# Expert weights loaded, waited for and released expert by expert

## What is computed

```
combine = jnp.sum(one_hot(expert_id, 16) * top_w[..., None], axis=1)
for e in range(N_EXPERTS):                       # 16 experts, 1024 -> 512 -> 1024
    he = jax.nn.silu(t @ w_gate[e]) * (t @ w_up[e])
    y = y + combine[:, e:e + 1] * (he @ w_down[e])
```

## Time and profile before

| | us |
|---|---|
| median of 3 runs | 702.59 |
| lowest and highest | 701.43, 703.89 |
| the profiled execution | 701.2 |
| its span | 699.4 |
| PE busy in the span | 662.6 (95%) |
| DVE, ACT busy | 298.5, 192.0 |

### The profile page before, as it was taken

How to read it: one execution, slowest core, us unless ns; L and a number is a source line. 1 busy time by engine, 2 the same in 40 slices (tenths; PEclk the granted TensorE clock), 3 DMA queues, 4 the chain that set the end, 5 groups by cost and what they waited for, 6 DMA issues and landing times.

```text
span 699.4 us, 9145 instructions
## 1 busy us (share of the span) xinstructions
PE 662.6 (95%) x3442; PEld 380.2 (54%) x3442; DVE 298.5 (43%) x632; ACT 192.0 (27%) x342; POOL 16.2 (2%) x29
## 2 busy tenths in 40 slices
PE   6999999999999999997999999999999999999883
PEld 5878778653444444431388878784543353352331
DVE  4478986611232122121474888673221322121234
ACT  3457543421111110100154554342201111111102
POOL 3100000200000000000020000000000000000000
PEclk9999999999999999999999999999999999999998
DMA  9985049999999999999986330998999999999991
GB/s 339 327 291 186 1 189 423 379 412 408 423 420 420 423 420 421 422 421 421 402 291 235 126 121 31 396 422 330 424 419 422 422 420 421 420 422 420 422 408 63
DMA packets 46027, 240.96 MB, mean 345 GB/s; under 512 B 3457, under 2 KB 3649, under 8 KB 21281
## 3 DMA queue, kind: packets, MB, share of 16 engines
q1 hardware_dynamic: 44800, 238.21, 84.2%
q0 software_dynamic: 1040, 2.04, 1.2%
q10 hardware_dynamic: 144, 0.13, 0.1%
HBM read 239.32 MB, written 1.05 MB: 344 GB/s over the span
## 4 chain that ended last, share of the span: by engine, by line
PE 75%; DMA 22%; DVE 1%; issue 1%; ACT 1%; DVEq 0%; SPq 0%
PE psum L1086 23%; PE psum L765 22%; DMA up_w<-in_w_up 21%; PE psum L1119 10%; PE psum L785 4%; PE psum L1066 3%; PE psum L1027 2%; PE psum L745 1%; PE psum L991 1%; PE psum L932 1%; DMA x<-in_x 1%; PE psum L1100 1%; PE psum L844 1%; PE psum L801 1%; PE psum L820 0%
## 5 line engine op out<-in xcount | busy, mean ns | idle before, releaser
L1086 PE MATMUL psum<-up_w,xT 128*64 128x512 f32 x512 | 114.2, 594 | 9.8 <-DMA up_w<-in_w_up 9.8
L1119 PE MATMUL psum<-down_w,scores 128*64 128x512 f32 x512 | 113.5, 595 | 0.0
L765 PE MATMUL psum<-piece_hi,hT_part 128*128 128x512 f32 x320 | 100.1, 394 | 0.0
L1086 PEld LDWEIGHTS psum<-up_w,xT 128*64 128x64 f32 x512 | 36.9, 137 | 83.7 <-issue 64.5
L1119 PEld LDWEIGHTS psum<-down_w,scores 128*64 128x64 f32 x512 | 36.6, 137 | 63.9 <-issue 61.6
L765 PEld LDWEIGHTS psum<-piece_hi,hT_part 128*128 128x128 f32 x320 | 59.0, 188 | 13.2 <-issue 1.7
L1523 DVE TENSOR_TENSOR y_lo<-psum,y_hi 128x512 fp32r<-128x512 f32 x32 | 22.1, 691 | 101.9 <-ACT y_hi L701 101.9
L765 PE MATMUL psum<-piece_lo,hT_part 128*128 128x512 f32 x160 | 62.4, 390 | 0.0
L1086 PE MATMUL psum<-gate_a,xT 128*64 128x512 f32 x256 | 56.9, 594 | 5.0 <-DMA gate_a<-in_w_gate 5.0
L1086 PE MATMUL psum<-gate_b,xT 128*64 128x512 f32 x256 | 56.4, 593 | 0.0
L1502 DVE SCALAR_TENSOR_TENSOR work<-work,psum 128x512 f32<-128x512 f32 x16 | 11.0, 687 | 105.2 <-ACT work L690 105.2
(11 more groups left out here) (243 smaller groups left out, 834.0 us busy)
## 6 DMA issues: line engine op xcount, KB each, us to landing
up_w<-in_w_up SPq DMA_DIRECT2D x32, 2048.0 KB, 17.2
down_w<-in_w_down SPq DMA_DIRECT2D x64, 1024.0 KB, 14.4
gate_b<-in_w_gate SPq DMA_DIRECT2D x32, 1024.0 KB, 14.4
gate_a<-in_w_gate SPq DMA_DIRECT2D x32, 1024.0 KB, 18.3
up_w<-in_w_in SPq DMA_DIRECT2D x6, 2048.0 KB, 13.2
down_w<-in_w_in SPq DMA_DIRECT2D x4, 2048.0 KB, 20.7
down_w<-in_w_out SPq DMA_DIRECT2D x4, 2048.0 KB, 8.1
up_w<-in_w_in SPq DMA_DIRECT2D x4, 1024.0 KB, 8.8
```

Source lines behind the costliest of these rows:

```text
L765: ins = pe.matmul(o, tokens, w[b][:, c, :], start=(c == 0 and n == 0), stop=(c == DC - 1 and n == len(parts) - 1))
L1086: ins = pe.matmul(psum[e * SLOTS:(e + 1) * SLOTS, bank, :], xT[:, c, k:k + SLOTS], w[:, e, c, :], start=(c == 0), stop=(c == DC - 1))
L1119: ins = pe.matmul(psum[e * SLOTS:(e + 1) * SLOTS, 2 + n, :], heT[:, c, e * SLOTS:(e + 1) * SLOTS], down_w[:, e, c, n * COLS:(n + 1) * COLS ...
```

## The change

`load_experts` takes the place of `load_halves`: one 2 MB transfer for one expert, with all of its contraction, 16 KB in a row per partition. The semaphores now count experts: `gate_loaded[o][e]`, `up_loaded[e]`, `down_loaded[e]` rise when expert e has landed, and `gated`, `upped`, `downed` when expert e has been used. PE runs all chunks of expert 0 and then all of expert 1: eight matmul instructions of one column half in a row, then eight of the other. For down the order is expert, column half n, chunk. Only the first four chunks of the gate product of item 0 keep the two experts alternating.

```diff
-        gate_loaded = [[signal(f"gate_loaded{o}{b}", 32) for b in range(2)] for o in range(2)]
-        up_loaded = [signal(f"up_loaded{b}", 16) for b in range(2)]
-        down_loaded = [signal(f"down_loaded{b}", 32) for b in range(2)]
+        gate_loaded = [[signal(f"gate_loaded{o}{e}", 16) for e in range(2)] for o in range(2)]
+        up_loaded = [signal(f"up_loaded{e}", 16) for e in range(2)]
+        down_loaded = [signal(f"down_loaded{e}", 16) for e in range(2)]
...
-                def load_halves(dst, src, loaded, used, g, q, back=0, halves=(0, 1), experts=(0, 1)):
-                    for b in halves:
+                def load_experts(dst, src, loaded, used, g, q, back=0, experts=(0, 1)):
+                    for e in experts:
                         if used is not None:
-                            sp.wait_ge(used.sem, used.at(g, b + 1 - back * used.turn))
+                            sp.wait_ge(used.sem, used.at(g, e + 1 - back * used.turn))
                             settle(sp)
-                        if dst is up_w:
-                            sp.dma_start(dst[:, :, 4 * b:4 * b + 4, :], src[bass.ds(q, 1), :, :, 4 * b:4 * b + 4, :]
-                                         .rearrange("q p e c n -> (q p) e c n")).then_inc(loaded[b].sem, 16)
-                            continue
...
-                        for e in experts:
-                            sp.dma_start(dst[:, e, part[0], part[1]], src[bass.ds(q, 1), :, e, part[0], part[1]]
-                                         .rearrange("q p c n -> (q p) c n")).then_inc(loaded[b].sem, 16)
+                        sp.dma_start(dst[:, e], src[bass.ds(q, 1), :, e].rearrange("q p c n -> (q p) c n")).then_inc(loaded[e].sem, 16)
...
-                        for c in range(DC):
-                            if bank == 0 and i % 2 == 0:
-                                tokens_ready(pe, g0, i // GROUP, i % GROUP // 2, c)
-                            if c % 4 == 0:
-                                pe.wait_ge(loaded[c // 4].sem, loaded[c // 4].at(turn_of, loaded[0].turn))
+                        def hidden(e, c):
+                            k = (i % GROUP) * P + e * SLOTS
+                            return pe.matmul(psum[e * SLOTS:(e + 1) * SLOTS, bank, :], xT[:, c, k:k + SLOTS],
+                                             w[:, e, c, :], start=(c == 0), stop=(c == DC - 1))
+                        begun = 0
+                        if bank == 0 and i == 0:
+                            begun = DC // 2
                             for e in range(2):
-                                k = (i % GROUP) * P + e * SLOTS
-                                ins = pe.matmul(psum[e * SLOTS:(e + 1) * SLOTS, bank, :], xT[:, c, k:k + SLOTS],
-                                                w[:, e, c, :], start=(c == 0), stop=(c == DC - 1))
-                            if c % 4 == 3:
-                                ins.then_inc(done.sem, 1)
+                                pe.wait_ge(loaded[e].sem, loaded[e].at(turn_of, 16))
+                            for c in range(begun):
+                                tokens_ready(pe, g0, 0, 0, c)
+                                for e in range(2):
+                                    hidden(e, c)
+                        for e in range(2):
+                            if begun == 0:
+                                pe.wait_ge(loaded[e].sem, loaded[e].at(turn_of, 16))
+                            for c in range(begun, DC):
+                                if bank == 0 and i % 2 == 0 and e == 0:
+                                    tokens_ready(pe, g0, i // GROUP, i % GROUP // 2, c)
+                                ins = hidden(e, c)
+                            ins.then_inc(done.sem, 1)
...
-                    for b in range(2):
-                        pe.wait_ge(down_loaded[b].sem, down_loaded[b].at(g0 + i, 32))
+                    for e in range(2):
+                        pe.wait_ge(down_loaded[e].sem, down_loaded[e].at(g0 + i, 16))
                         for n in range(2):
-                            if b == 0:
+                            if e == 0:
                                 pe.wait_ge(y_lo_ready.sem, y_lo_ready.item(g0, i, n - 1))
-                            for c in range(2 * b, 2 * b + 2):
-                                for e in range(2):
-                                    ins = pe.matmul(psum[e * SLOTS:(e + 1) * SLOTS, 2 + n, :], heT[:, c, e * SLOTS:(e + 1) * SLOTS],
-                                                    down_w[:, e, c, n * COLS:(n + 1) * COLS], start=(c == 0), stop=(c == HC - 1))
+                            for c in range(HC):
+                                ins = pe.matmul(psum[e * SLOTS:(e + 1) * SLOTS, 2 + n, :], heT[:, c, e * SLOTS:(e + 1) * SLOTS],
+                                                down_w[:, e, c, n * COLS:(n + 1) * COLS], start=(c == 0), stop=(c == HC - 1))
```

More of the change, by code:

```diff
@@ L437, in _ @@
                 sp.wait_ge(projected.sem, projected.at(l, BV + 1))
-                load_halves(up_w, up_d, up_loaded, upped, first, l * PAIRS, 1)
+                load_experts(up_w, up_d, up_loaded, upped, first, l * PAIRS, 1)
                 sp.wait_ge(attended.sem, attended.at(l, 2))
                 settle(sp)
-                load_halves(gate_w[0], gate_d, gate_loaded[0], None, None, l * PAIRS)
-                load_halves(gate_w[1], gate_d, gate_loaded[1], None, None, l * PAIRS + 1, experts=(0,))
+                load_experts(gate_w[0], gate_d, gate_loaded[0], None, None, l * PAIRS)
+                load_experts(gate_w[1], gate_d, gate_loaded[1], None, None, l * PAIRS + 1, experts=(0,))
                 for n in range(2):
@@ L446, in _ @@
                     settle(sp)
-                    load_halves(down_w, down_d, down_loaded, None, None, l * PAIRS, experts=(n,))
+                    load_experts(down_w, down_d, down_loaded, None, None, l * PAIRS, experts=(n,))
                     if n == 0:
-                        load_halves(gate_w[1], gate_d, gate_loaded[1], None, None, l * PAIRS + 1, experts=(1,))
+                        load_experts(gate_w[1], gate_d, gate_loaded[1], None, None, l * PAIRS + 1, experts=(1,))
                 sp.wait_ge(items_ready.sem, items_ready.at(l, 1))
@@ L458, in load_gate @@
                 def load_gate(g, o):
-                    load_halves(gate_w[o], gate_d, gate_loaded[o], gated, g, pair(g), 2)
+                    load_experts(gate_w[o], gate_d, gate_loaded[o], gated, g, pair(g), 2)
                 def load_up(g):
-                    load_halves(up_w, up_d, up_loaded, upped, g, pair(g), 1)
+                    load_experts(up_w, up_d, up_loaded, upped, g, pair(g), 1)
                 def load_down(g):
-                    load_halves(down_w, down_d, down_loaded, downed, g, pair(g), 1)
+                    load_experts(down_w, down_d, down_loaded, downed, g, pair(g), 1)
                 load_gate(first + 2, 0)
@@ L1111, in item @@
                     pe.wait_ge(heT_ready.sem, heT_ready.item(g0, i, 1))
-                    for b in range(2):
-                        pe.wait_ge(down_loaded[b].sem, down_loaded[b].at(g0 + i, 32))
+                    for e in range(2):
+                        pe.wait_ge(down_loaded[e].sem, down_loaded[e].at(g0 + i, 16))
                         for n in range(2):
-                            if b == 0:
+                            if e == 0:
                                 pe.wait_ge(y_lo_ready.sem, y_lo_ready.item(g0, i, n - 1))
-                            for c in range(2 * b, 2 * b + 2):
-                                for e in range(2):
-                                    ins = pe.matmul(psum[e * SLOTS:(e + 1) * SLOTS, 2 + n, :], heT[:, c, e * SLOTS:(e + 1) * SLOTS],
-                                                    down_w[:, e, c, n * COLS:(n + 1) * COLS], start=(c == 0), stop=(c == HC - 1))
+                            for c in range(HC):
+                                ins = pe.matmul(psum[e * SLOTS:(e + 1) * SLOTS, 2 + n, :], heT[:, c, e * SLOTS:(e + 1) * SLOTS],
+                                                down_w[:, e, c, n * COLS:(n + 1) * COLS], start=(c == 0), stop=(c == HC - 1))
                             if n == 1:
                                 ins.then_inc(downed.sem, 1)
-                            elif b == 1:
+                            elif e == 1:
                                 ins.then_inc(y_summed.sem, 1)
```

## The result

The changed kernel takes 878.99 us (median of 4 runs, 878.62 to 880.0) against 702.72 us for the kernel before, a ratio of 1.2511 (95% interval 1.2487 to 1.2536). The forecast was 707 us, 697 to 716. What came is the rival "PE passes over few waiting records", at 879 in place of the 930 us worked out for it.

What follows compares the result with a forecast made beforehand. The prediction took weight transfers at about 420 GB/s to set each layer's end. Later starts, longer rows and tail summed to +2.0 us in layer 0 and +2.7 in layer 1, +4.7 on 702.59: 707 us, range 697 to 716.

Steps and rivals of the forecast that it cites:

- PE passes over few waiting records: Rival on PE's order: only three waiting pairs passed, so runs of 16 barely overlap; +230 us, 930 us; chance 0.11.
- What a run of eight of one expert costs: Step on PE's matmuls: one expert alone takes 6.9 us, unless PE looks far enough ahead to the other expert.
- I take the deep one: Choice on PE's look-ahead: fifteen waiting instructions can be passed, so loaded experts run side by side at no cost; forecast's chance 0.58.
- Strict order: Rival on PE's order: matmuls start in program order, only a run's last record overlaps; about 985 us; chance 0.04.
- The pairs are the two passes of one instruction: Rival on PE: column halves do not matter, a lone expert needs 3.4 us for eight instructions; 697 us; chance 0.07.
- Gain of longer rows: Term on weight transfers: 16 KB rows save 2%, 0.095 us on each 4.97; -3.4 us in layer 0, -3.6 in layer 1.
- No gain: Rival on weight transfers: longer rows do not raise the rate, the -7.0 us is lost; 714 us; chance 0.13.
- much faster rows: Rival on weight transfers: more than 0.16 us saved on each; at 0.2 the sum is -3.5, 699 us; chance 0.05.
- The tail: Term after up's last landing: all of expert 1's work remains, 6.9 us, so +3.4 us in each layer.
- The stream starts later: Term at gate(2), the first load waiting for a release: it goes out later, +2.0 us in layer 0, +3.2 in layer 1.
- The later loads of the first items at 0, at worst 1.5 a layer: Term on loads after gate(2): they just find their buffers free, costing 0, at worst another 1.5 us a layer.

Runs made afterwards that it cites:

- the kernel with loads alone: Changed kernel's transfers and releases by expert, but PE waits for both experts and then alternates them chunk by chunk: 718.99 us, ratio 1.0238.
- the kernel with the first items by halves: Against the 718.99 us kernel (loads by expert, PE alternating): gate(2), up of items 1 to 3, down of 1 and 3 by halves; 708.07 us.

## Why the prediction was wrong

The step that failed is the choice in "What a run of eight of one expert costs": "I take the deep one". Everything ahead of it held. The records do go two at a time because neighbours lie in two column halves, an expert alone takes 0.43 us a record, and line 1039 does show that at least three waiting pairs are passed. But "nothing hints that three is a limit, since all that there was to pass was passed" took a lack of evidence for evidence: where only three are waiting, a limit of three and one of sixty look the same, and the whole change hung on whether fifteen can be passed. What the runs showed in its place is a limit of three: at 208.19, at the other borders of the runs of 16, and with records of half the length. 0.11 for "few passed over" was too little for a case against which no row spoke.

The rival's own sum was 50 us too high by two terms. With three passed, the other half starts beside the 13th record, so a run costs 12 steps (5.15 us), not 13. And I let down end before the next gate: gate of the next item overlaps down's last run in the same way (208.19). An item became 36.27 us, not 39.4.

*Strict order* (985 us) falls with the row at 208.19: a matmul starts before three older ones. The Trainium skill ("TensorE: Matmul & The Clock Gate", section "The mechanism") has matmuls start and end strictly in program order; this trace does not agree. *The pairs are the two passes of one instruction* falls too: a lone expert's 16 records take 0.43 us each.

The four terms of the sum could be read only with PE's order put back, in the kernel with loads alone:

- *Gain of longer rows*: 4.90 us for 2 MB in place of 4.97, 1.4 to 1.6%. I took 2%. Right, and far from the ends of its range. "No gain" and "much faster rows" are both out.
- *The tail*: +3.4 a layer, right to 0.1 us (339.61 against 336.21, in the kernel with the first items by halves), but without the clock: a wait for both experts leaves PE idle for 2.7 us, and in layer 0 the lower clock behind it took another 1.4.
- *The stream starts later*: by the landing times gate(2)'s first 2 MB came 3.0 us later in layer 0 and, against the start of item 0's gate, 3.5 in layer 1, for +2.0 and +3.2. gate(2) went out 4.2 us later in layer 0, 0.7 of it because item 0's gate began at 135.99, not 135.25.
- *The later loads of the first items at 0, at worst 1.5 a layer*: wrong, +5.6 and +2.8. I had written that up(g+1) goes out 20 us after up(g) has landed. For up(3) it was 9 us, and 4 in the kernel before; with the later release the queue ran dry ahead of it.

With these the forecast's +4.7 becomes 6.5 - 5.7 + 8.4 + 6.8 + 1.4 = +17.4 (start, rows, gaps, tail, clock), for 17.3 between the two profiled executions (718.53 and 701.2) and 16.4 between the medians. The kernel whose first items go by halves came to 708.07 us, next to the 707 forecast. That is no success of the forecast, which was for another kernel.

## What to carry to other kernels

If two column halves of the array are to work side by side, put their matmuls in turn: with matmuls like these, a run of one half may be at most four records (two float32 instructions), or eight where a lag of four steps does not matter. Where a trace shows that n things were passed because there were only n, the limit is unknown; do not count "nothing was late" as evidence, and when the whole change hangs on the answer, measure it by the order alone first. Before a release is made coarser, follow every load of a single-buffered tile in the first items: a late release costs nothing only while the queue holds other transfers.

## What the runs showed of the hardware

- PE starts a matmul of one column half ahead of at most three older waiting records of the other half (208.19 and 257.85). It holds at 1.3 us of waiting work (records of 512 columns) and at 0.64 us (256 columns), and the two passes of one float32 instruction count as two.
- 2 MB in rows of 16 KB take 4.90 us, in rows of 8 KB 4.97.
- In the middle of a stage, idle times of PE of 2.25 to 3.53 us were followed by a granted clock of 0.50 in some cases (2.25 us: a product of 8.70 us; 2.32: 8.78; 2.71: 8.48; 3.53: 10.03), and in others not (2.24, 2.69 and 3.00 us: 7.09). So the length of the wait alone does not decide; what does is open. In the kernel before, whose waits were 1.3 us, the clock did not fall.
